# Stick-breaking attention in pairs of units: scores and scans of two units first, values one pair later, ring of four

## The chip, the cores and the metric

The kernel runs on one core of one Trainium2 chip. The metric is the device time of one execution in microseconds, as the median of several runs.

## What is computed

One layer of a streaming encoder for two requests that share the weights: a prompt of 1024 rows, and a sample of 64 new rows with 512 rows of cached keys and values. The layer is: modulation rows from a conditioning vector; a normed projection into u, q, k, v; a pooling mixer on u; stick-breaking attention with 8 heads of 64; an output projection with residual and two layer norms; a router; a mixture of 16 experts with a second residual and norm. Attention, cut to what matters:

```python
z = einsum('bqhd,bkhd->bhqk', qi, k) * scale            # scores
valid = (k_pos[None, :] < pi[:, None])[None, None]      # strictly causal
log_beta = log_sigmoid(z)
log_1m = where(valid, log_sigmoid(-z), 0.0)
suffix = cumsum(log_1m, axis=3, reverse=True) - log_1m
a = where(valid, exp(log_beta + suffix), 0.0)
attn = einsum('bhqk,bkhd->bqhd', a, v)
...
mix = concatenate([pool_out, attn], axis=-1) @ w_out
x = layer_norm(ALPHA * x + (1 + g1) * mix, ln1_g, ln1_b)
hn2 = (norm(x) * (1 + sc2) + sh2)
```

## The kernel before, in words

Three blocks follow one another: block_a (modulation, norm, projection), block_b (attention, output projection, first norm, router logits) and block_c (routing and experts). The change lies in block_b.

**How attention is computed.** The kernel doesn't form logarithms. ScalarE takes sigmoid(-z/8), which is 1 minus the stick's fraction; VectorE multiplies it up by a scan from the last key backwards (`tensor_tensor_scan`), which gives the stick that is left at each key. The weight of a key is the difference of two neighbours of that product, and the kernel moves this difference onto the values: dv holds v of a row minus v of the row before, so that left-over sticks times dv, plus the last v (vlast), is the attention.

**Units.** attention_units() lists 56 units in order: units 0 to 7 are the sample tile (per pair of heads one unit of 64 new keys and one of 512 cached ones), 8 to 23 the prompt tiles 0 to 3 with one unit for each of 4 pairs of heads (128, 256, 384, 512 keys), and 24 to 55 the tiles 4 to 7 with two units each: the upper piece (top, 128 to 512 keys, masked) and then the lower one (bottom, 512 keys), whose scan starts from what the upper left. Each unit does both heads (h = 0, 1) of its pair.

**Steps of unit u.** On TensorE (PE) scores(u) (L994) into banks 2(u%2)+h; on ScalarE (ACT) sticks(u), the sigmoid (L1135), into ring[u % RING]; on VectorE (DVE) weights(u), two scans in place (L1267 masked top, L1269 otherwise); on PE turn(u) (L1009), transposes of both heads, in blocks of 128 keys, into banks 4 and 5; on ACT copy_aT(u) (L1151), one copy a head; on PE values(u) (L1028), one matmul for each head and 128 keys, into bank 6 over the one or two units of a tile and pair of heads; on DVE, behind the last of these, copy_att(u) (L1277), with vlast added. Waits: turn(u) waits for left_ready (scan of u) and, head by head, for aT_copied of the unit before; values(u) waits for aT_copied of u and, for a top unit, for att_copied of the accumulation before; sticks(u) waits for the transposes of u - RING and for a scan.

**Order.** One loop over u on each engine, LAG = 2. PE: scores(u), turn(u-2), the other work of u, values(u-3). ACT: sticks(u), copy_aT(u-2), other work. DVE: weights(u), copy_att(u-3), other work. The other work is written out by hand in the tables PE_BESIDE, ACT_BESIDE, DVE_BESIDE, a list of steps for each u; each engine runs its own list strictly in order. The steps are: TV:n/DV (transposes of v's differences, L981, and their DVE copy L1284), PM:n (pooling map, L973, ACT copy L1140), wh:n and wl:n (high and low part of w_out, L1156 on ACT and L1289 on DVE), Ph:n and Pl:n (the same of the mixed rows, L1165, L1294), M0:n and M1:n (the halves of the output projection, 24 matmuls each, L1040), C0:n and C1:n (their DVE copies, L1305), R:n on DVE (residual, L1317), E, G, B (norm and modulation, L1325, L1341, L1358), Q1 and Q2 on ACT (squares, L1178), T0:n and T1:n (transposes of hn2, L1049, copied by H0 and H1, L1187), T2:n and R:n on PE (router, L1059 and L1068, copied by H2 on ACT and L:n on DVE, L1367), KT:n (keys transposed for output). Up to u = 57 all PE steps of the tables write bank 7 (`take` waits for the reader of the step before); in the last list (u = 58) all eight banks are used. At u = 0 and 1 PE also does turn_v(4) to (8) and DVE and ACT stage_v (v staged for output, L1237).

The lists of TensorE and the first of ScalarE (those of VectorE stand in the diff):

```python
PE_BESIDE = {
    1: "TV:0", 3: "PM:0", 4: "PM:1", 5: "TV:1", 7: "TV:2", 9: "TV:3", 10: "TV:4", 12: "TV:5", 14: "TV:6", 15: "TV:7",
    16: "TV:8", 17: "PM:2", 18: "PM:3", 19: "PM:4", 20: "PM:5", 21: "PM:6", 22: "PM:7", 23: "PM:8", 24: "PM:9",
    25: "PM:10", 26: "PM:11", 28: "M0:0", 29: "M1:0", 31: "M0:1", 33: "M1:1", 34: "T0:0", 35: "M0:2", 36: "T1:0",
    37: "M1:2", 38: "T2:0", 39: "R:0", 40: "M0:3", 41: "T0:1", 42: "M1:3", 43: "T1:1", 44: "M0:4", 45: "T2:1",
    46: "M1:4", 47: "R:1", 48: "M0:5", 49: "T0:2", 50: "T1:2", 51: "M1:5", 52: "T2:2", 53: "M0:6", 54: "R:2",
    55: "M1:6", 56: "T0:3", 57: "M0:7",
    58: "T1:3 M1:7 T2:3 T0:4 M0:8 R:3 T1:4 M1:8 T2:4 T0:5 KT:0 R:4 T1:5 KT:1 KT:2 T2:5 KT:3 KT:4 R:5 T0:6 KT:5 T1:6 KT:6 KT:7 T2:6 KT:8 R:6 T0:7 T1:7 T2:7 T0:8 T1:8 R:7 T2:8 R:8",
...
ACT_BESIDE = {
    3: "PM:0", 4: "PM:1", 12: "wh:0", 13: "wh:1", 14: "wh:2", 15: "wh:3", 16: "wh:4", 17: "PM:2 wh:5",
    18: "wh:6 PM:3", 19: "wh:7 PM:4", 20: "PM:5", 21: "PM:6", 22: "PM:7", 23: "PM:8", 24: "PM:9", 25: "PM:10",
...
```

## Time and profile before

| | us |
|---|---|
| median of 3 runs | 864.76 (864.37 to 865.07) |
| the profiled execution | 863.53 |
| span of its records | 861.8 |
| TensorE matmul busy | 792.0 (92%), 4805 matmuls |
| VectorE busy | 597.8 (69%) |
| ScalarE busy | 349.7 (41%) |
| GpSimd busy | 314.2 (36%) |
| mean granted TensorE clock | 0.968 of full speed |

The profile is one execution. Times in it are microseconds from the start of the span. Attention runs from about 243 us (first sigmoid) to 494 us (last values), the last of the output projection and the router to 533 us, then routing and experts to the end. A row of the timeline is: start, duration (several instructions merged, with their count x), engine, line, operation, tiles written and read, shapes, and in brackets how long the engine was idle before it and what ended that. The ends of matmuls are modelled, so that a group overlaps the next by some hundredths of a microsecond; the step from start to start is the surer figure.

### The profile page before, as it was taken

Reading aid. Unit: us, or ns where it says so; the run is one execution under the profiler, and the core shown is the slowest. Engines: PE = TensorE matmul, PEld = TensorE weight load, DVE = VectorE, ACT = ScalarE, POOL = GpSimd, SP = SyncE. Lnnn points to the kernel's source line nnn. Section 1 sums busy time; section 2 is a strip of 40 time slices with the busy share of each in tenths; the row PEclk is TensorE's granted clock in tenths of the full one; section 3 lists DMA queues with packets and bytes.
Section 4 is the critical chain, followed back from the end, with each engine's and each line's share of the span. In section 5 each row is a group of like instructions: output and inputs, shape, how many; then the busy total and the mean of one; then the engine's idle time right before and its main releaser. Section 6 shows DMA issues by size and latency. Waiting matters only on the chain. (4 is left out here: it accounts for less than half of the span.)

```text
span 861.8 us, 13448 instructions
## 1 busy us (share of the span) xinstructions
PE 792.0 (92%) x4805; PEld 625.4 (73%) x4806; DVE 597.8 (69%) x685; ACT 349.7 (41%) x645; POOL 314.2 (36%) x259
## 2 busy tenths in 40 slices
PE   3899999999978899999999995599999999999894
PEld 2689999999945566766767784378888888888641
DVE  6679679852079965875777566998557998563097
ACT  3811110111156763444444435544544444444144
POOL 3000799960000001000000001257665897663156
PEclk9999999999999999999999996699999999999897
DMA  8956544630073501321102037798779998889594
GB/s 322 397 175 204 163 152 132 200 98 2 1 257 144 144 17 50 100 72 38 62 26 74 25 122 265 279 327 278 272 253 334 401 384 289 278 306 345 175 355 157
DMA packets 77362, 165.32 MB, mean 192 GB/s; under 512 B 7397, under 2 KB 32517, under 8 KB 75266
## 3 DMA queue, kind: packets, MB, share of 16 engines
q1 hardware_dynamic: 68402, 132.15, 44.2%
q0 software_dynamic: 7760, 28.31, 9.3%
q10 hardware_dynamic: 1152, 4.19, 1.4%
q8 instruction: 32, 0.52, 0.3%
q14 instruction: 16, 0.13, 0.0%
HBM read 132.57 MB, written 32.08 MB: 191 GB/s over the span
## 5 line engine op out<-in xcount | busy, mean ns | idle before, releaser
L2101 PE MATMUL psum<-we_hi,x_parts 128*128 x384 | 137.5, 403 | 1.4 <-DVE we_lo L1724 1.1
L1724 DVE TENSOR_TENSOR we_lo<-we_raw,we_hi 128x2048 fp32r<-128x2048 f32 x48 | 116.1, 2422 | 1.5
L1723 DVE CAST we_hi<-we_raw 128x2048 fp32r<-128x2048 f32 x44 | 60.7, 1379 | 47.9 <-DMA we_raw<-in_w_down_dram 24.5
L449 PE MATMUL psum<-hn_hi,w_hi 128*128 128x364 f32 (+1 forms) x384 | 90.7, 331 | 1.3 <-issue 0.7
L449 PE MATMUL psum<-hn_lo,w_hi 128*128 128x364 f32 (+1 forms) x384 | 90.1, 329 | 0.0
L449 PE MATMUL psum<-hn_hi,w_lo 128*128 128x364 f32 (+1 forms) x384 | 89.9, 328 | 0.0
L2101 PEld LDWEIGHTS psum<-we_hi,x_parts 128*128 128x128 f32 x384 | 72.1, 188 | 16.5 <-issue 2.3
L1040 PE MATMUL psum<-wo_hi,mixin 128*128 128x512 f32 (+1 forms) x256 | 83.2, 396 | 0.6 <-DVE logits L1367 0.6
L2101 PE MATMUL psum<-we_lo,x_parts 128*128 x192 | 75.2, 392 | 0.0
L633 DVE SCALAR_TENSOR_TENSOR proj<-wm,cT,proj 128x2048 f32<-128x2048 f32 x28 | 72.6, 2638 | 0.1
L449 PEld LDWEIGHTS psum<-hn_hi,w_hi 128*128 128x128 f32 x384 | 67.0, 189 | 5.7 <-issue 4.8
L449 PEld LDWEIGHTS psum<-hn_hi,w_lo 128*128 128x128 f32 x384 | 67.6, 189 | 0.0
L449 PEld LDWEIGHTS psum<-hn_lo,w_hi 128*128 128x128 f32 x384 | 67.4, 189 | 0.0
L929 POOL TENSOR_TENSOR rs_x<-var_x,mhalf 128x1 f32<-128x1 f32 (+1 forms) x9 | 13.0, 1448 | 147.7 <-DVE var_x L1325 147.7
L526 ACT ACTIVATE bias<-psum 128x2 f32<-128x2 f32 x16 | 2.8, 172 | 157.1 <-PE psum L449 157.1
L1135 ACT ACTIVATE ring<-psum 128x1024 f32<-128x1024 f32 (+5 forms) x56 | 44.1, 787 | 49.2 <-PE psum L994 47.1
L1267 DVE TENSOR_TENSOR_SCAN ring<-ring,mask 128x128 f32<-128x128 f32 (+4 forms) x72 | 50.9, 747 | 9.0 <-ACT ring L1135 8.9
L1009 PEld LDWEIGHTS psum<-ident,ring 128*128 128x128 f32 (+2 forms) x328 | 34.4, 142 | 30.8 <-issue 24.0
L1821 POOL DMA_INDIRECT ff_d<-yst,idsy x24 | 50.7, 2111 | 15.6 <-ACT yst L1944 6.7
L1040 PEld LDWEIGHTS psum<-wo_hi,mixin 128*128 128x128 f32 (+1 forms) x256 | 46.3, 181 | 12.5 <-issue 1.0
L1269 DVE TENSOR_TENSOR_SCAN ring<-ring 128x512 f32<-128x512 f32 (+1 forms) x40 | 49.1, 1267 | 7.3 <-ACT ring L1135 7.3
L1040 PE MATMUL psum<-wo_lo,mixin 128*128 128x512 f32 (+1 forms) x128 | 49.9, 390 | 0.0
(334 smaller groups left out, 1587.3 us busy)
## 6 DMA issues: line engine op xcount, KB each, us to landing
we_raw<-in_w_up_dram SPq DMA_DIRECT2D x32, 1024.0 KB, 8.4
wm<-in_w_mod_dram SPq DMA_DIRECT2D x16, 1024.0 KB, 5.3
we_raw<-in_w_down_dram SPq DMA_DIRECT2D x16, 1024.0 KB, 6.6
w_raw<-in_w_in_dram SPq DMA_DIRECT2D x16, 512.0 KB, 6.2
we_raw<-ff_d SPq DMA_DIRECT2D x12, 512.0 KB, 8.3
proj<-in_x_prompt_dram SPq DMA_DIRECT2D x4, 1024.0 KB, 8.1
sc_room<-in_w_mod_dram SPq DMA_DIRECT2D x4, 1024.0 KB, 14.0
proj<-in_w_mod_dram SPq DMA_DIRECT2D x2, 2048.0 KB, 12.2
```

The costliest lines, as they stand in the source:

```text
L449: mm = pe.matmul(psum[:, 3 * slot + c, 0:n], w[:, slot, k, :], hn[:, k, t0:t0 + n], start=(k == 0 and w is w_hi and hn is hn_hi), stop=(k ...
L633: ins = dve.scalar_tensor_tensor(out=out, in0=w, scalar=c, in1=out, op0=ALU.mult, op1=ALU.add)
L929: pool.tensor_tensor(rs[of][0:r, n:n + 1], var[of][0:r, n:n + 1], mhalf[0:r, 0:1], ALU.pow).then_inc(rstd_ready[of], 1)
L1009: mm = pe.transpose(psum[0:m, 4 + h, b:b + r], ring[0:r, s, h, b:b + m], ident[0:r, 0:r])
L1040: mm = pe.matmul(out[0:r, :], mix_room(n)[:, part, k, 0:r], w[:, k, 512 * half:512 * half + 512], start=(k == 0 and part == 0 and w is wo_ ...
L1135: act.activation(ring[0:r, u % RING, :, 0:n], psum[0:r, 2 * s:2 * s + 2, 0:n], ACT.Sigmoid, scale=-0.125).then_inc(stay_ready, 1)
L1267: ins = dve.tensor_tensor_scan(w, w, mask[0:r, end - n:end][:, ::-1], first, ALU.mult, ALU.max)
L1269: ins = dve.tensor_tensor_scan(w, w, w, first, ALU.mult, ALU.bypass)
L1723: then(dve.tensor_copy(we_hi[:, a:b], raw))
L1724: dve.tensor_tensor(we_lo[:, a:b], raw, we_hi[:, a:b].bitcast(F32), ALU.subtract).then_inc(ready, 1)
L1821: pool.indirect_dma_start(ff_d, bass.IndirectOffsetOnAxis(idsy[:, s:s + 1], 0), yst[:, s, :], None).then_inc(scattered[s], 16)
L2101: mm = pe.matmul(psum[:, bank, :], x[:, s, k, :], w[:, bass.ds(at + k * 2 * DE, 2 * DE)], start=(k == 0 and x is x_hi and w is we_hi), sto ...
```

## The change

- The loops of PE and ACT go over even u and treat two units at once. PE: scores(u), scores(u+1), values(u-4), values(u-3), turn(u-2), the other work of u and of u+1, turn(u-1). ACT: sticks(u), sticks(u+1), copy_aT(u-2), other work of both, copy_aT(u-1). DVE: at even u weights(u), weights(u+1), copy_att(u-4), copy_att(u-3), then the other work of u; at odd u other work alone.
- RING goes from 3 to 4. The room comes from junk, which now shares wp's room, and zeros, which is a part of mask (one memset and one count of CONSTS less).
- The odd ones of units 8 to 23 sum their values in bank 5 (att_bank), all others in bank 6. turn(u), head 1, waits for att_copied of the odd unit before the pair where that unit used bank 5; a top unit's values wait for the last accumulation in the same bank (bank_read).
- wl:0 to wl:7 on DVE are spread over units 13 to 23; they were in 12 to 19.
- turn_v(4) to (8) follow scores(1); stage_v(8) follows stage_v(6).

```diff
@@ -143,7 +143,7 @@
         with ExitStack() as mid:
             proj = mid.enter_context(nc.sbuf_tensor("proj", [P, FC, NT], F32))
             utail = mid.enter_context(nc.sbuf_tensor("utail", [P, 4, 2, HIST], F32))
-            wp = mid.enter_context(nc.sbuf_tensor("wp", [P, 4, P], F32))
+            wp, junk = rooms(nc, mid, ("wp", [P, 4, P], F32), ("junk", [P, KC, P], BF16))
             psc = mid.enter_context(nc.sbuf_tensor("psc", [P, 4], F32))
             wgr = mid.enter_context(nc.sbuf_tensor("wgr", [P, KC, 32], F32))
             old_room = mid.enter_context(nc.sbuf_tensor("old_room", [P, 2, D], F32))
@@ -689,7 +689,7 @@
 
 UNITS = len(attention_units())
 ORDER = (PT,) + tuple(range(PT))
-RING = 3
+RING = 4
 LAG = 2
 
 
@@ -712,8 +712,8 @@
     57: "Q2:6 Ph:8 H1:3 H2:3 H0:4 Q1:7 Q2:7 H1:4 H2:4 H0:5 KT:0 H1:5 Q1:8 H2:5 KT:1 KT:2 H0:6 KT:3 H1:6 KT:4 Q2:8 H2:6 KT:5 KT:6 KT:7 H0:7 KT:8 H1:7 H2:7 H0:8 H1:8 H2:8",
 }
 DVE_BESIDE = {
-    2: "TV:0", 3: "DV:0", 5: "TV:1", 7: "TV:2", 9: "TV:3", 10: "TV:4", 12: "TV:5 wl:0", 13: "wl:1 TV:6 wl:2",
-    14: "wl:3", 15: "TV:7", 16: "TV:8 wl:4", 17: "wl:5", 18: "wl:6", 19: "wl:7", 26: "Pl:0", 28: "C0:0",
+    2: "TV:0", 3: "DV:0", 5: "TV:1", 7: "TV:2", 9: "TV:3", 10: "TV:4", 12: "TV:5", 13: "wl:0",
+    14: "TV:6", 15: "wl:1 TV:7", 16: "TV:8 wl:2", 17: "wl:3", 18: "wl:4", 19: "wl:5", 21: "wl:6", 23: "wl:7", 26: "Pl:0", 28: "C0:0",
     29: "C1:0 R:0 Pl:1", 30: "E1:0 G1:0", 31: "B1:0 C0:1 E2:0 G2:0", 32: "B2:0", 33: "C1:1 R:1 Pl:2", 34: "E1:1 G1:1",
     35: "B1:1 C0:2 E2:1", 36: "G2:1 B2:1", 37: "C1:2 R:2 Pl:3", 38: "E1:2", 39: "L:0 G1:2", 40: "B1:2 E2:2 C0:3",
     42: "C1:3 R:3 Pl:4", 43: "G2:2 E1:3 B2:2 G1:3", 44: "B1:3 C0:4", 45: "E2:3", 46: "C1:4 R:4 Pl:5 L:1", 47: "E1:4",
@@ -752,9 +752,8 @@
         k_room, mixin = one_room(nc, ctx, [P, 2, KC, P], ("k_room", F32), ("mixin", F32R))
         lT = sb("lT", [P, P])
         gather = sb("gather", [P, 32])
-        junk = sb("junk", [P, KC, P], BF16)
         mask = sb("mask", [P, 512])
-        zeros = sb("zeros", [P, P])
+        zeros = mask[:, 0:P]
         vlast = sb("vlast", [P, 4, TILES])
         edge = sb("edge", [P, 4, 2])
         sums = [sb("sums_x1", [P, TILES]), sb("sums_hn2", [P, TILES])]
@@ -813,7 +812,7 @@
         gather_made = 1
         sample_units = sum(u[0] == PT for u in units)
         EVEN = 112
-        CACHE_LOADS, EARLY_STORES, CONSTS = 16 * 4, 16 * (TILES + 2), 5
+        CACHE_LOADS, EARLY_STORES, CONSTS = 16 * 4, 16 * (TILES + 2), 4
         K_FIRST = 6
         ACT_TILES, DVE_TILES = TILES // 2, TILES - TILES // 2
 
@@ -832,6 +831,15 @@
         def v_staged(n):
 
             return (act_staged, n // 2 + 1) if n % 2 else (dve_staged, n // 2 + 1)
+
+        def att_bank(u):
+
+            return 5 if units[u][5] and units[u][6] and u % 2 else 6
+
+        def bank_read(u):
+
+            q = units[u][7]
+            return max((v[7] + 1 for w, v in enumerate(units[:u]) if v[7] < q and att_bank(w) == att_bank(u)), default=0)
 
         def mod_row(dst, b, part):
             return dst, mod_d[b, part * D:(part + 1) * D].partition_broadcast(P)
@@ -1004,6 +1011,8 @@
                 for h in range(2):
                     if u >= 1:
                         pe.wait_ge(aT_copied, 2 * u - 1 + h)
+                    if h and u >= LAG and att_bank(u - 1 - u % 2) == 5:
+                        pe.wait_ge(att_copied, units[u - 1 - u % 2][7] + 1)
                     for b in range(0, n, P):
                         m = min(P, n - b)
                         mm = pe.transpose(psum[0:m, 4 + h, b:b + r], ring[0:r, s, h, b:b + m], ident[0:r, 0:r])
@@ -1017,15 +1026,15 @@
                     pe.wait_ge(old_ready, 1)
                 else:
                     pe.wait_ge(dv_copied, ORDER.index(i) + 1)
-                if top and q:
-                    pe.wait_ge(att_copied, q)
+                if top and bank_read(u):
+                    pe.wait_ge(att_copied, bank_read(u))
                 nb = -(-n // P)
                 for b in range(nb):
                     m = min(P, n - b * P)
                     v = dv_old[0:m, b, :] if old else dv[0:m, s0 // P + b, :]
                     for h in range(2):
                         c = p * P + 64 * h
-                        mm = pe.matmul(psum[64 * h:64 * h + 64, 6, 0:r], v[:, c:c + 64], aT[0:m, s, h, b, 0:r],
+                        mm = pe.matmul(psum[64 * h:64 * h + 64, att_bank(u), 0:r], v[:, c:c + 64], aT[0:m, s, h, b, 0:r],
                                        start=(top and b == 0), stop=(bottom and b == nb - 1))
                 mm.then_inc(pv_done, 1)
 
@@ -1077,16 +1086,7 @@
 
             for n in range(4):
                 turn_v(n)
-            for u in range(nu + LAG + 1):
-                if u < nu:
-                    scores(u)
-                if 0 <= u - LAG < nu:
-                    turn(u - LAG)
-                if u >= nu:
-                    values(u - LAG - 1)
-                if u < 2:
-                    for n in ((4, 5, 6), (7, 8))[u]:
-                        turn_v(n)
+            def others(u):
                 if u == nu + LAG:
                     last_reader.update({b: [(stay_ready, nu)] for b in range(4)})
                     last_reader.update({b: [(aT_copied, 2 * nu)] for b in (4, 5)})
@@ -1106,8 +1106,28 @@
                         turn_k(n)
                     else:
                         router(n)
-                if LAG < u < nu:
-                    values(u - LAG - 1)
+
+            for u in range(0, nu + LAG, 2):
+                if u < nu:
+                    scores(u)
+                    scores(u + 1)
+                if u >= 2 * LAG:
+                    values(u - 2 * LAG)
+                    values(u - 2 * LAG + 1)
+                if u == 0:
+                    for n in range(4, TILES):
+                        turn_v(n)
+                if u >= LAG:
+                    turn(u - LAG)
+                others(u)
+                if u < nu:
+                    others(u + 1)
+                if u >= LAG:
+                    turn(u + 1 - LAG)
+            values(nu - 2)
+            values(nu - 1)
+            others(nu + 1)
+            others(nu + LAG)
 
         @block.scalar
         def _(act):
@@ -1198,13 +1218,7 @@
                 act.wait_ge(pv_done, nu)
                 act.activation(dv[0:rows(t), t, :], bank("KT", t)[0:rows(t), :], ACT.Copy).then_inc(act_staged, 1)
 
-            for u in range(nu + LAG + 1):
-                if u < nu:
-                    sticks(u)
-                if 0 <= u - LAG < nu:
-                    copy_aT(u - LAG)
-                if u < 2:
-                    stage_v(5 + 2 * u)
+            def others(u):
                 for step, n in beside(ACT_BESIDE, u):
                     if step == "PM":
                         copy_pool(n)
@@ -1221,6 +1235,23 @@
                     else:
                         copy_h(n, int(step[1]))
 
+            for u in range(0, nu + LAG, 2):
+                if u < nu:
+                    sticks(u)
+                    sticks(u + 1)
+                if u == 0:
+                    stage_v(5)
+                    stage_v(7)
+                if u >= LAG:
+                    copy_aT(u - LAG)
+                others(u)
+                if u < nu:
+                    others(u + 1)
+                if u >= LAG:
+                    copy_aT(u + 1 - LAG)
+            others(nu + 1)
+            others(nu + LAG)
+
         @block.vector
         def _(dve):
             step_ = Tally(b_dve)
@@ -1274,7 +1305,7 @@
                 i, p = units[u][0], units[u][1]
                 r = rows(i)
                 dve.wait_ge(pv_done, u + 1)
-                dve.tensor_scalar(proj[:, 4 + p, i * P:i * P + r], psum[:, 6, 0:r], vlast[:, p, i:i + 1], None,
+                dve.tensor_scalar(proj[:, 4 + p, i * P:i * P + r], psum[:, att_bank(u), 0:r], vlast[:, p, i:i + 1], None,
                                   ALU.add).then_inc(att_copied, 1)
 
             def copy_dv(n):
@@ -1367,15 +1398,18 @@
                 dve.tensor_tensor(logits[0:r, ORDER[n], :], bank("R", n)[0:r, 0:NLOG], blog[0:r, :], ALU.add).then_inc(logits_copied, 1)
 
             for u in range(nu + LAG + 1):
-                if u == 1:
-                    stage_v(8)
-                if u < nu:
-                    weights(u)
-                if u > LAG and units[u - LAG - 1][6]:
-                    copy_att(u - LAG - 1)
+                if u % 2 == 0:
+                    if u < nu:
+                        weights(u)
+                        weights(u + 1)
+                    if u >= 2 * LAG:
+                        for before in (u - 2 * LAG, u - 2 * LAG + 1):
+                            if units[before][6]:
+                                copy_att(before)
                 if u == 0:
                     stage_v(4)
                     stage_v(6)
+                    stage_v(8)
                 if u == 1:
                     dve.wait_ge(cache_loaded, CACHE_LOADS)
                     dve.tensor_tensor(dv_old[:, :, :], v_sh, dv_old[:, :, :], ALU.subtract).then_inc(old_ready, 1)
```

## Rows read from the trace of the kernel before

**Rows 1.** The page's slices: busy tenths of TensorE in 40 equal parts of the span.

```profile
PE   3899999999978899999999995599999999999894
```

**Rows 2.** Stretches of 10 us, core 0: length, PE, PEld, DVE, ACT, POOL busy, clock, DMA.

```profile
282.00:292.00 10.00, 8.93 (x70) 5.13 (x66) 10.00 (x15) 7.24 (x14) 0.00 (x0) 1.00 0.51 141
...
302.00:312.00 10.00, 10.00 (x86) 6.63 (x86) 6.86 (x11) 6.94 (x12) 0.59 (x1) 1.00 0.08 23
```

**Rows 3.** Waits of TensorE in 243 to 300 us: total, times, longest.

```profile
PE psum L1028 <- DVE proj L1277: 3.3, 4, 1.9
```

**Rows 4.** Waits of TensorE in 300 to 478 us.

```profile
PE psum L1049 <- DVE proj L1305: 3.9, 2, 2.0
PE psum L1040 <- DVE logits L1367: 0.6, 1, 0.6
PE psum L1059 <- DVE proj L1305: 0.5, 1, 0.5
```

**Rows 5.** Timeline of TensorE at several places of attention.

```profile
277.51 0.44 PE L1028 MATMUL psum<-aT_room,dv 128*64 128x128 f32 x4 [1.06 <-DVE proj L1277]
...
293.03 1.02 PE L973 MATMUL psum<-proj,wp 128*128 128x512 f32 x2
...
321.03 0.46 PE L1040 MATMUL psum<-wo_hi,mixin 128*64 128x512 f32 x1
...
397.98 0.47 PE L1040 MATMUL psum<-wo_hi,mixin 128*128 128x512 f32 x1
...
403.64 1.09 PE L1028 MATMUL psum<-aT_room,dv 128*64 128x128 f32 x16
...
404.67 1.13 PE L994 MATMUL psum<-proj 64*128 64x512 f32 x4
```

**Rows 6.** Timeline of VectorE: scans, low_wo and copy_att (272.69 is unit 12, 322.31 unit 28).

```profile
272.69 1.27 DVE L1267 TENSOR_TENSOR_SCAN ring<-ring,mask 128x256 f32<-128x256 f32 x2 [0.60 <-ACT ring L1135]
...
274.72 1.22 DVE L1289 TENSOR_TENSOR wo_lo<-wo_raw,wo_hi 128x1024 fp32r<-128x1024 f32 x1
...
277.04 0.33 DVE L1277 TENSOR_SCALAR proj<-psum,vlast 128x128 f32<-128x128 f32 x1
...
284.73 1.79 DVE L1267 TENSOR_TENSOR_SCAN ring<-ring,mask 128x384 f32<-128x384 f32 x2
...
297.69 2.33 DVE L1267 TENSOR_TENSOR_SCAN ring<-ring,mask 128x512 f32<-128x512 f32 x2
...
313.82 2.46 DVE L1269 TENSOR_TENSOR_SCAN ring<-ring 128x512 f32<-128x512 f32 x2 [1.77 <-ACT ring L1135]
...
322.31 0.71 DVE L1267 TENSOR_TENSOR_SCAN ring<-ring,mask 128x128 f32<-128x128 f32 x2
```

**Rows 7.** Timeline of ScalarE in 290 to 297 us: wo_hi, pooling copy, aT copies, sigmoid.

```profile
290.87 1.10 ACT L1156 ACTIVATE wo_hi<-wo_raw 128x1024 fp32r<-128x1024 f32 x1
291.82 0.73 ACT L1140 ACTIVATE proj<-psum,psc 128x512 f32<-128x512 f32 x1
...
293.14 0.88 ACT L1151 ACTIVATE aT_room<-psum 128x384 f32<-128x384 f32 x2
...
295.96 1.03 ACT L1135 ACTIVATE ring<-psum 128x1024 f32<-128x1024 f32 x1 [0.42 <-PE psum L994]
```

**Rows 8.** Stretches of 2 us at two gaps of TensorE, columns as in group 2.

```profile
393.00:395.00 2.00, 0.33 (x4) 0.10 (x1) 0.63 (x4) 1.81 (x3) 0.30 (x1) 1.00 0.43 130
395.00:397.00 2.00, 1.64 (x16) 1.14 (x16) 1.84 (x3) 1.80 (x4) 0.25 (x1) 1.00 0.44 133
442.00:444.00 2.00, 0.10 (x2) 0.07 (x2) 1.78 (x5) 0.69 (x1) 0.00 (x0) 1.00 0.00 0
446.00:448.00 2.00, 2.00 (x7) 0.63 (x4) 1.96 (x2) 1.43 (x3) 0.00 (x0) 0.50 0.00 0
```

**Rows 9.** Timeline of TensorE, 442 to 453 us.

```profile
443.96 0.63 PE L1049 MATMUL psum<-ident,old_room 128*128 128x128 f32 x4 [1.90 <-DVE proj L1305]
...
445.37 2.08 PE L994 MATMUL psum<-proj 64*128 64x512 f32 x4
```

More of the change, by code:

```diff
@@ L155, in build @@
             block_b(nc, ident, mhalf, psum, proj, utail, logits, fixed, mod_d, x1_d, hn2_d, x_prompt,
-                    x_sample, cache_v, old_room, wp, psc, wgr, blog, vprev, w_out, ln1_g, ln1_b,
+                    x_sample, cache_v, old_room, wp, junk, psc, wgr, blog, vprev, w_out, ln1_g, ln1_b,
                     k_prompt, v_prompt, pool_prompt, k_sample, v_sample, pool_sample)
@@ L734, in block_b @@
 def block_b(nc, ident, mhalf, psum, proj, utail, logits, fixed, mod_d, x1_d, hn2_d, x_prompt, x_sample,
-            cache_v, old_room, wp, psc, wgr, blog, vprev, w_out, ln1_g, ln1_b,
+            cache_v, old_room, wp, junk, psc, wgr, blog, vprev, w_out, ln1_g, ln1_b,
             k_prompt, v_prompt, pool_prompt, k_sample, v_sample, pool_sample):
@@ L901, in _ @@
             pool.memset(v_sh[0:1, 0, :], 0.0).then_inc(b_const, 1)
-            pool.memset(zeros[:, :], 0.0).then_inc(b_const, 1)
             pool.memset(logits[:, PT, :], 0.0).then_inc(b_const, 1)
```

## The prediction

> **What bounds the kernel now.** I read four views. First the page's 40 slices [rows 1]: TensorE is at nine tenths almost everywhere, and its one soft place before the routing is in the slices after 240 us, where attention starts. Then stretches of attention [rows 2]: from 282 to 292 us VectorE is busy 10.0 of 10 us and TensorE 8.9; from 302 us on TensorE is at 10.0 and VectorE at 6.9. So units 12 to 19 are paced by VectorE and the later ones by TensorE. The waits say the same: in 243 to 300 us TensorE waited 3.3 us for the copy of finished attention, L1277 [rows 3]; in 300 to 478 us its largest wait is 3.9 us, transposes (L1049) that found PSUM bank 7 not yet copied [rows 4]. What an exchange of order can win is thus small: 5 us of idle after 300 us, and TensorE's own cost of switching from one kind of work to the next.
>
> **Durations.** Start to start on TensorE, a unit with 512 keys takes 1.03 us for values (403.64 to 404.67) and 1.06 for scores (the transposes follow at 405.73); two pooling matmuls take 0.95, a mix half of 24 matmuls 5.66 (397.98 to 403.64) [rows 5]. VectorE, two scans: 1.19 us (256 keys), 1.71 (384), 2.25 (512, masked), 2.38 (unmasked), 0.65 (128); a step of low_wo 1.14; copy_att 0.33, start to start 0.24; copy_dv 0.66 [rows 6]. ScalarE: sigmoid 0.92 start to start (512 keys), 0.7 (384), 0.5 (256); aT copy of a head 0.28, 0.4 and 0.5; wo_hi 1.0, pooling copy 0.7 [rows 7]. A hop from VectorE to TensorE: the copy at 277.04 ends at 277.37, the values it held start at 277.51: 0.14 us [rows 5, 6]. From TensorE to another engine: about 0.28 us after the last column.
>
> **The change, part by part.**
>
> *A new wait in units 12 to 27.* The odd unit of each pair of 8 to 23 now sums its values in bank 5, the bank of head 1's transposes. So turn(u-2), head 1, waits for copy_att(u-3). TensorE comes to it right behind values(u-4) and values(u-3); but VectorE issues that copy only behind weights(u) and weights(u+1), the four scans of the pair whose scores TensorE has just made. Queued behind the waiting transpose are both units' other work, turn(u-1) and scores(u+2), for which the next scans wait. So each engine waits for the other once a pair, for u = 12, 14, ... 26. A round, from scan(u) to scan(u+2), is: four scans, two copies and the hop; then head 1's transposes, others(u), others(u+1), turn(u-1), scores(u+2), sigmoid(u+2). On ScalarE the aT copy, its own other steps and the aT copies of u-1 stand ahead of that sigmoid.
>
> Pair 20 worked out: scans 4.5, copies 0.57, hop 0.14: 5.2 us. Head 1 (three blocks of 107 ns) to 5.5; PM:5, its copy behind the aT copy, then PM:6, all in bank 7, to 7.6; turn(19) 0.84, scores(22) 1.06, 0.11 to the sigmoid, 1.05 to the scan: 10.65. Pair 12: 3.1 to head 1, aT copy to 3.65, wo_hi:0 and :1 to 5.65, two aT copies 0.35, sigmoid 0.63: 6.6. Pair 14: 3.3 after head 1, TV:6, its copy and TV:7 to 5.3, turn(13) and scores(16) to 6.85, sigmoid: 7.8. Pair 16: 4.3, then on ScalarE wo_hi, the copy of PM:2 behind TV:8, wo_hi to 7.65, aT copies and sigmoid: 9.05. Pair 18: 4.45, aT copy, wo_hi, copy of PM:3 to 6.8, PM:4 to 7.9, turn(17) 0.84, scores(20) 1.06, 1.16: 11.0. Pairs 22 and 24, with two pooling steps each: 10.1 and 10.1. Pair 26, with one and Ph:0: 7.5. Sum 72.8 us. In the kernel before, scan(12) starts at 272.69 and scan(28) at 322.31: 49.6 us for the same eight pairs [rows 6]. **+23.2.** With none of the other work in the round the rounds sum to 55, so +5 is the lower bound.
>
> *Before unit 12.* Two scans (2.8 us) now stand ahead of stage_v(4), which frees the bank for turn_v(8); low_wo's eight steps are spread over units 13 to 23 in place of 12 to 19; the large steps remain. **+0.8**, bounds -1 and +2, from no start that moves by more than a scan.
>
> *The hand-over.* Before, M0:0 starts 1.3 us ahead of scan(28), at 321.03 [rows 5, 6]. Now scores(29), values(24), values(25) and turn(26) stand between, and it starts 2.1 us behind: +3.4, less scores(29), 1.1, which is done early: **+2.3**.
>
> *Fewer switches, units 28 to 55.* Scores are 4 passes of 213 ns, 0.85 us, and take 1.06 start to start; values are 16 times 54 ns, 0.86, and take 1.03 [rows 5]. A switch to or from a kind that uses half of the array costs 0.16 to 0.21 us. A pair had six or seven of them and has three or four: I take 0.5 us a pair, 14 pairs: **-7**, bounds 0 and -9. In units 12 to 27 that gain lies in idle time. The Trainium skill (TensorE: Matmul & The Clock Gate, Step-by-step: what each phase is for) says that TensorE pulls weight loads ahead of running matmuls; if that hid every switch, this term would be 0. The rows show a cost between kinds all the same.
>
> *Other work by two, one bank.* Mix halves, transposes of hn2 and router steps all take bank 7. Between two of them stood values, scores and a turn, 3 us; now others(u) and others(u+1) are adjacent and the second waits for the reader of the first. After a mix half with a step behind it: 0.28 + 0.68 + 0.14 = 1.1, for pairs 28, 40, 42, 46, 48: 5.5. Pair 44, where VectorE reaches C0:4 late, behind B1:3: 1.5. T0:0 then M0:2 (34) waits for aT copy, square (1.25) and copy_h (0.5): 2.1; T2:0 then R:0 (38) and T2:2 then M0:6 (52) the same way, 2.1 and 1.8; T1 then M1 (36, 50) for copy_h alone, 0.9 and 1.0; R:2 then M1:6 (54) for copy_logits, now behind four scans of 4.8 us: 2.6. Sum 17.5, in place of the present 3.9 + 0.6 + 0.5 [rows 4]: **+12.5**, bounds +5 and +15.
>
> *Free edits.* zeros as a part of mask saves one memset on GpSimd, idle there. junk shares wp's room; its first write (unit 30) is behind wp's last use (unit 26). A ring of four lets sigmoid(u+1) go ahead, which the pairs need. Square's load of the next x rows, SP's loads and stores keep their order, with microseconds of slack; the tail behind M0:7 and the expert stage move as a block.
>
> *Clock.* From 442 to 444 us TensorE is busy 0.10 of 2 us, and at 446 to 448 the granted clock is 0.50 (1.2 GHz); the gap at 393 to 395, 0.33 of 2 us busy, is followed by 1.00 [rows 8]. In the first case scores at 445.37 span 2.08 us against 1.13 at full clock [rows 5, 9]. Each of the eight rounds has a gap of 2 to 3.5 us; in half of them I take a fall, 1 us each, as TensorE streams half of the round: **+4**, bounds 0 and +15. The skill's same page (Why this matters for your kernels) advises against idle gaps between bursts, which speaks against this change.
>
> **Sum.** 0.8 + 23.2 + 2.3 - 7 + 12.5 + 4 = +35.8. Against the profiled execution (span 861.8, 863.5 with what lies around it) that is 899.3, against the median 864.8 it is 900.6. I say 900.
>
> **Rivals.**
> *Light rounds* (0.22): the engines overlap more of each round than I give, the clock stays full, the bank waits are near their lower bound: 0.8 + 12 + 2.3 - 7 + 8 = +16, 881. For it: ScalarE has a third of its time free. Against: each engine's order is fixed.
> *Half clock all through* (0.13): the gaps leave TensorE at 1.2 GHz over most rounds, and bank waits bring falls of their own: +50, 915. For it: the scores at 445.37. Against: the gap at 393.
> *Switches win* (0.06, faster): if bank 5 is copied before TensorE reaches head 1's transposes, the rounds cost nothing and the gain on switches stays, with 4 us of bank waits in place of 5: 864.8 - 8 = 857. It decides where the four scans (2.4 to 4.8 us) end before scores, two values and one head (1.7 to 3.7 us); by the scan rows they don't in any of the pairs.
> *Not what it says* (0.02, within 0.2%): switches aren't saved and waits only change names: 865.
> The forecast itself has 0.57.
>
> **How the numbers follow.** The range may leave out 2 in 10: 877 to 918 holds the forecast, most of the light rounds and over half of the half-clock case. A measurement of this kernel tells about 0.2% (1.7 us) from no change. Faster 0.06, same 0.02, slower 0.92.
>
> **What would show it.** After: TensorE idle ahead of L1009 in eight places 7 to 11 us apart, ended by VectorE's copy_att; scan(12) to scan(28) near 73 us; scores of two units as one run of 8 matmuls, 1.9 us for 512 keys; waits ahead of L1040 and L1049 of about 1 us each for the readers of bank 7; tail and experts as long as before. I am wrong if those L1009 waits sum to under 10 us, or if units 28 to 55 take less time than before.

## The result: 5.9% slower

The changed kernel takes 914.8 us (median; 913.1 to 918.4), the kernel before 864.6: the ratio is 1.0589, 95% interval 1.0571 to 1.0607. The forecast was 900, range 877 to 918. The profiled execution of the changed kernel has a span of 916.6 us, 54.8 more than that of before; it is the longest one of four, so the stages below, which are cut from it, add up to 4.7 us more than the medians differ by.

In the changed kernel the lines are: scores L1001, transposes L1018, values L1037, mix L1049, hn2 transposes L1058, router L1068 and L1077, pooling map L980, sigmoid L1155, scans L1298 and L1300, copy_att L1308, copy_dv L1315, C0 and C1 L1336.

The page's slices of the changed kernel, to be laid beside [rows 1]:

```profile
PE   3899999999777768999898989469999999999894
...
DVE  6779498820375554577666637699845999664077
...
PEclk9999999999976679999999999779999999999897
```

The digits 6 to 8 of TensorE from the eleventh slice on (229 to 366 us) hold units 0 to 27 of attention; the kernel before has one 7 and two 8 there. VectorE is at 3 to 7: neither is the bound, each waits for the other. The granted clock falls to 6 and 7 tenths. Behind it TensorE is at eight and nine tenths, up to the 4 and the 6 of the routing. Two stretches of these units, up to unit 12 and units 12 to 27 (columns as in [rows 2], clock the third last):

```profile
243.00:282.00 39.00, 28.69 (x220) 18.30 (x220) 26.76 (x40) 15.35 (x39) 0.00 (x0) 0.74 0.48 182
282.00:364.00 82.00, 58.83 (x350) 35.94 (x352) 43.86 (x61) 38.80 (x68) 2.21 (x10) 0.77 0.16 42
```

The span cut at four events that both traces show (start of scan(12) and of scan(28) on VectorE, of M0:0 and M0:7 on TensorE; scan(u) is the start of unit u's scans, all in us; a negative time means that M0:0 starts first):

| stage | before | after | more | forecast |
|---|---|---|---|---|
| start to scan(12) | 272.7 | 281.9 | +9.2 | +0.8 |
| scan(12) to scan(28), eight rounds | 49.6 | 82.2 | +32.5 | +23.2, and +4 for the clock |
| scan(28) to M0:0 | -1.3 | 1.2 | +2.4 | +3.4 |
| M0:0 to M0:7 | 166.6 | 178.1 | +11.4 | +4.4 (12.5 - 7 - 1.1) |
| M0:7 to the end | 374.1 | 373.4 | -0.8 | 0 |

**The rounds.** The round of u = 20 in the changed kernel, all engines (unit 20's scans start at 321.09, unit 22's at 334.33):

```profile
321.09 4.57 DVE L1298 TENSOR_TENSOR_SCAN ring<-ring,mask 128x512 f32<-128x512 f32 x4 [6.84 <-ACT ring L1155]
...
325.58 0.58 DVE L1308 TENSOR_SCALAR proj<-psum,vlast 128x128 f32<-128x128 f32 x2
...
326.31 0.87 PE L1018 MATMUL psum<-ident,ring 128*128 128x128 f32 x3 [3.53 <-DVE proj L1308]
...
327.61 0.31 ACT L1160 ACTIVATE proj<-psum,psc 128x64 f32<-128x64 f32 x1
...
327.97 2.08 PE L980 MATMUL psum<-proj,wp 128*128 128x512 f32 x2 [0.46 <-ACT proj L1160]
...
329.84 1.49 PE L1018 MATMUL psum<-ident,ring 128*128 128x128 f32 x6
...
331.25 2.83 PE L1001 MATMUL psum<-proj 64*128 64x512 f32 x8
...
333.27 1.94 ACT L1155 ACTIVATE ring<-psum 128x1024 f32<-128x1024 f32 x2 [1.42 <-PE psum L1001]
...
334.33 2.34 DVE L1298 TENSOR_TENSOR_SCAN ring<-ring,mask 128x512 f32<-128x512 f32 x2 [7.03 <-ACT ring L1155]
```

It is the order of the forecast, step by step: four scans; copy_att twice, the last to 326.16; head 1's transposes at 326.31 after 3.53 us of idle; the copy of PM:5; PM:6; turn(19); scores(22) and (23); the sigmoid; the scan. 13.2 us, where I had worked out 10.65. What is longer are TensorE's steps alone: PM:6 1.87 from start to start in place of 0.95, turn(19) 1.41 for 0.84, scores to sigmoid 2.0 for 1.2. They run at 1.2 GHz: the granted clock of 326 to 333 us is 0.51. The waits of TensorE in 282 to 364 us:

```profile
PE psum L1018 <- DVE proj L1308: 18.7, 8, 3.5
PE psum L980 <- ACT proj L1160: 2.8, 4, 0.8
```

Eight waits for copy_att, one for each round, 1.7 to 3.5 us each and 18.7 us in all, as in the list of what would show it. They end 6.5 to 14 us apart.

**Units 28 to 55.** TensorE's waits in 365 to 543 us; [rows 4] has the same of before with 5.0 us in all:

```profile
PE psum L1058 <- DVE proj L1336: 4.0, 3, 2.3
PE psum L1049 <- ACT old_room L1207: 3.2, 3, 1.8
PE psum L1049 <- DVE logits L1398: 2.6, 1, 2.6
PE psum L1037 <- ACT aT_room L1171: 2.5, 5, 0.9
PE psum L1077 <- ACT lT L1214: 1.6, 1, 1.6
PE psum L1049 <- ACT lT L1214: 1.5, 1, 1.5
PE psum L1068 <- DVE proj L1336: 1.1, 1, 1.1
PE psum L1077 <- DVE proj L1336: 0.9, 1, 0.9
PE psum L1049 <- DVE old_room L1336: 0.9, 1, 0.9
```

Their sum is 18.3 us. Twelve of them, 15.8 us, are the twelve pairs of adjacent steps in bank 7 that the forecast lists, with 2.6 for the router's copy behind four scans (M1:6), as worked out. The other five, 2.5 us, are values (L1037) that wait for their aT copy; the forecast has no such wait. The switches are saved as well:

```profile
507.71 1.99 PE L1001 MATMUL psum<-proj 64*128 64x512 f32 x8
509.63 1.97 PE L1037 MATMUL psum<-aT_room,dv 128*64 128x128 f32 x32
511.53 0.66 PE L1018 MATMUL psum<-ident,ring 128*128 128x128 f32 x4
```

Scores of two units with 512 keys take 1.92 us from start to start, twice 1.06 before; values 1.90, twice 1.03 before [rows 5].

### The profile page after: what moved, and what is told of

It reads as the page before. It is cut to its first block and busy times, and to the rows that moved or that the text cites. A ratio compares the mean times of both kernels' runs of the same rounds, so it can differ in the third digit from the quotient of the medians.

```text
span 916.6 us, 13462 instructions
## 1 busy us (share of the span) xinstructions
PE 809.7 (88%) x4805; PEld 642.2 (70%) x4806; DVE 601.7 (66%) x685; ACT 354.8 (39%) x645; POOL 310.6 (34%) x258
## 5 line engine op out<-in xcount | busy, mean ns | idle before, releaser
L1049 PE MATMUL psum<-wo_hi,mixin 128*128 128x512 f32 (+1 forms) x256 | 84.4, 401 | 8.2 <-ACT old_room L1207 3.2
L1298 DVE TENSOR_TENSOR_SCAN ring<-ring,mask 128x128 f32<-128x128 f32 (+4 forms) x72 | 50.2, 746 | 53.6 <-ACT ring L1155 53.6
L633 DVE SCALAR_TENSOR_TENSOR proj<-wm,cT,proj 128x2048 f32<-128x2048 f32 x28 | 72.5, 2636 | 0.5 <-DMA wm<-in_w_mod_dram 0.5
L1018 PE MATMUL psum<-ident,ring 128*128 128x128 f32 (+2 forms) x328 | 52.6, 298 | 18.7 <-DVE proj L1308 18.7
L1171 ACT ACTIVATE aT_room<-psum 128x512 f32<-128x512 f32 (+4 forms) x112 | 47.3, 460 | 52.0 <-PE psum L1018 51.5
L1018 PEld LDWEIGHTS psum<-ident,ring 128*128 128x128 f32 (+2 forms) x328 | 39.7, 156 | 32.5 <-issue 29.1
L1049 PEld LDWEIGHTS psum<-wo_hi,mixin 128*128 128x128 f32 (+1 forms) x256 | 47.1, 184 | 21.2 <-issue 9.6
L1300 DVE TENSOR_TENSOR_SCAN ring<-ring 128x512 f32<-128x512 f32 (+1 forms) x40 | 49.2, 1270 | 8.1 <-ACT ring L1155 6.7
```

The lines of the kernel that those rows point to most:

```text
L633: ins = dve.scalar_tensor_tensor(out=out, in0=w, scalar=c, in1=out, op0=ALU.mult, op1=ALU.add)
L1018: mm = pe.transpose(psum[0:m, 4 + h, b:b + r], ring[0:r, s, h, b:b + m], ident[0:r, 0:r])
L1049: mm = pe.matmul(out[0:r, :], mix_room(n)[:, part, k, 0:r], w[:, k, 512 * half:512 * half + 512], start=(k == 0 and part == 0 and w is wo_ ...
L1171: act.activation(aT[0:m, s, h, 0:nb, 0:r], src, ACT.Copy).then_inc(aT_copied, 1)
L1298: ins = dve.tensor_tensor_scan(w, w, mask[0:r, end - n:end][:, ::-1], first, ALU.mult, ALU.max)
L1300: ins = dve.tensor_tensor_scan(w, w, w, first, ALU.mult, ALU.bypass)
```

## The experiments

All are edits of the changed kernel; their diffs are shortened, and ... marks what is left out. First what each came to, in us; the texts below were written before each ran. The last three columns are from one profiled execution each: the start of scan(12), the time from scan(12) to scan(28) (the eight rounds) and the time from M0:0 to M0:7.

| run | median | ratio to before (95%) | scan(12) | rounds | M0:0 to M0:7 |
|---|---|---|---|---|---|
| before | 864.6 | | 272.7 | 49.6 | 166.6 |
| the change | 914.8 | 1.059 (1.057 to 1.061) | 281.9 | 82.2 | 178.1 |
| e1_between | 887.4 | 1.027 (1.023 to 1.031) | 278.4 | 60.2 | 172.4 |
| e2_warm | 916.5 | 1.059 (1.056 to 1.062) | 282.3 | 83.3 | 176.4 |
| e3_split | 893.0 | 1.034 (1.032 to 1.035) | 277.2 | 73.9 | 164.3 |
| e4_pm | 912.5 | 1.055 (1.052 to 1.059) | 280.4 | 80.0 | 174.8 |
| e5_warm2 | 905.0 | 1.044 (1.039 to 1.048) | 279.8 | 71.3 | 174.8 |
| e6_all | 871.3 | 1.007 (1.004 to 1.009) | 276.4 | 54.4 | 163.2 |
| e7_vfirst_all | 881.9 | 1.017 (1.012 to 1.021) | 281.2 | 52.9 | 172.0 |
| e8_vfirst | 917.7 | 1.058 (1.054 to 1.063) | 281.0 | 60.8 | 197.4 |
| e9_hybrid | 861.4 | 0.996 (0.994 to 0.998) | 273.0 | 50.3 | 163.3 |
| e10_hybrid_adj | 875.0 | 1.010 (1.007 to 1.014) | 272.0 | 49.6 | 178.1 |
| e11_warm_all | 902.1 | 1.043 (1.040 to 1.047) | 275.7 | 72.5 | 176.4 |
| e12_hybrid_split | 863.3 | 0.999 (0.997 to 1.000) | 272.4 | 49.6 | 164.3 |

**Is it the copy behind four scans?** e1_between puts it between them:

```diff
                     if u < nu:
                         weights(u)
-                        weights(u + 1)
                     if u >= 2 * LAG:
...
                                 copy_att(before)
+                    if u < nu:
+                        weights(u + 1)
```

> The changed kernel with one exchange on VectorE: the two copies of finished attention stand between the scans of u and those of u+1, not behind both. Theory A (each round of units 12 to 27 is held by scans, then copy, then head 1's transposes): every round gets shorter by about one unit's scans (1.2, 1.2, 1.7, 1.7, 2.25, 2.25, 1.2, 1.2 us), 12.7 us, and by 3 to 6 more where the gap no longer halves the clock: 894 to 902 us; idle of TensorE ahead of L1018 falls from 18.7 us to under 8. Theory B (the rounds are long because TensorE runs at 1.2 GHz and ScalarE's other steps stand ahead of the sigmoid; the copy is not what is waited for): within 3 us of 914.8.

887.4: 27 us less, more than either number. The rounds are 21.9 us shorter, and their granted clock is 0.94 in place of 0.77. Theory B is out. How much of the 21.9 the copy gave and how much the clock, this run alone can't tell. With e5_warm2 (below), whose rounds take 71.3 us at 0.98 in the order of the change, it can: 11.0 us (71.3 - 60.2) for the copy's place, for 12.7 worked out, and 10.9 for the clock (with 0.98 and 0.94 neither run is quite at full clock, so both are estimates).

**What does the clock cost?** e2_warm fills TensorE's gaps with spare matmuls whose result nobody reads:

```diff
+                for _ in range(WARM.get(u, 0)):
+                    for sm, value in last_reader.get(7, ()):
+                        pe.wait_ge(sm, value)
+                    pe.matmul(psum[:, 7, :], ident[:, :], mask[:, :], start=True, stop=True)
                 if u >= LAG:
                     turn(u - LAG)
```

> The changed kernel with 41 spare matmuls of 512 columns (0.43 us each at full clock, bank 7, their result is overwritten unread) put into TensorE's gaps ahead of turn(u-2) in the rounds of u = 12 to 26, at most 3 us a round; everything else is as in the changed kernel. If the half clock in the rounds is a cost of its own beside the waits: the granted clock in 283 to 363 us rises from about 0.75 to over 0.9, and scan(12) to scan(28) falls from 82.2 us toward the 72.8 us of the forecast: 904 to 908 us. If the clock costs nothing there (the chain goes through VectorE and ScalarE): 914 to 917, or some us more where a spare matmul delays the transposes.

The clock rose to 1.00 in 283 to 363 us, and the time was 916.5. Taken by itself that would have said that the clock is free. But the trace showed each spare matmul at 0.87 us, twice what I had reckoned: those of u = 20 ended 2.0 us behind the copy that the transposes wait for, and stood in the round themselves. The next run has 18 of them in place of 41 (2 a round, 3 for u = 20 and 22):

> As the run with 41 spare matmuls, but with 18 (2 a round, 3 for u = 20 and 22), each 0.87 us by the last trace, so that they end before the copy that the transposes wait for. In the last run the spare matmuls of u = 20 ended 2.0 us behind the copy, which hid what the clock gives. If the half clock costs time of its own in the rounds (about 1 us each by the forecast, 2.4 us in the round of u = 20 by the trace): clock over 0.9 in 283 to 363 us and scan(12) to scan(28) of 70 to 76 us in place of 82.2: 902 to 909 us. If it costs nothing: 913 to 917.

905.0, and the rounds take 71.3 us, both as expected. Granted clock and busy time of 280 to 351 us, and the round of u = 20 again, now with TensorE at full clock (L1124 are the spare matmuls, copy_att is L1313, the pooling map L981, transposes L1019, scores L1002):

```profile
280.00:351.00 71.00, 60.32 (x382) 34.58 (x380) 43.79 (x61) 37.30 (x68) 2.88 (x10) 0.98 0.19 49
```

```profile
313.63 4.62 DVE L1303 TENSOR_TENSOR_SCAN ring<-ring,mask 128x512 f32<-128x512 f32 x4 [4.44 <-ACT ring L1160]
...
314.78 2.84 PE L1124 MATMUL psum<-mask,ident 128*128 128x512 f32 x6
...
318.17 0.57 DVE L1313 TENSOR_SCALAR proj<-psum,vlast 128x128 f32<-128x128 f32 x2
...
318.89 0.52 PE L1019 MATMUL psum<-ident,ring 128*128 128x128 f32 x3 [0.95 <-DVE proj L1313]
...
320.20 1.13 PE L981 MATMUL psum<-proj,wp 128*128 128x512 f32 x2 [0.61 <-ACT proj L1165]
...
321.16 0.82 PE L1019 MATMUL psum<-ident,ring 128*128 128x128 f32 x6
...
321.91 1.99 PE L1002 MATMUL psum<-proj 64*128 64x512 f32 x8
...
324.14 2.34 DVE L1303 TENSOR_TENSOR_SCAN ring<-ring,mask 128x512 f32<-128x512 f32 x2 [4.26 <-ACT ring L1160]
```

From scan to scan it is 10.51 us; the forecast's sum for it was 10.65. The eight rounds, by the starts of their scans:

| pair | 12 | 14 | 16 | 18 | 20 | 22 | 24 | 26 | sum |
|---|---|---|---|---|---|---|---|---|---|
| forecast | 6.6 | 7.8 | 9.05 | 11.0 | 10.65 | 10.1 | 10.1 | 7.5 | 72.8 |
| e5_warm2 | 6.4 | 7.6 | 9.1 | 10.7 | 10.5 | 9.8 | 9.9 | 7.2 | 71.3 |
| the change | 6.5 | 9.4 | 10.2 | 13.1 | 13.2 | 12.2 | 10.4 | 7.2 | 82.2 |

Each was sized rightly for the full clock, within 0.3 us, and the half clock adds 10.9 us (82.2 - 71.3).

**Ahead of unit 12.** The trace of the changed kernel at units 1 to 5 (L962 is turn_v(8), L1268 the copies of stage_v):

```profile
248.75 1.11 PE L962 MATMUL psum<-ident,proj 128*128 128x128 f32 x4 [3.54 <-DVE wo_raw L1268]
...
251.97 1.92 PE L1001 MATMUL psum<-k_room,proj 64*64 64x512 f32 x4
...
254.99 2.45 DVE L1300 TENSOR_TENSOR_SCAN ring<-ring 64x512 f32<-64x512 f32 x2 [1.82 <-ACT ring L1155]
257.36 0.66 DVE L1315 COPY dv<-psum 64x512 f32<-64x512 f32 x1
...
258.07 2.07 PE L980 MATMUL psum<-proj,wp 128*128 128x512 f32 x2 [3.83 <-DVE dv L1315]
...
260.08 1.11 PE L1018 MATMUL psum<-ident,ring 64*128 64x64 f32 x8
...
261.12 0.48 PE L1001 MATMUL psum<-proj 64*64 64x64 f32 x4
```

The first new wait is that of turn_v(8), 3.54 us for stage_v(4), which now stands behind the scans of units 0 and 1; in the kernel before turn_v waits 0.3. scores(2) and scores(3) stand behind it, and scores(3) starts at 251.97, in the kernel before at

```profile
248.43 1.08 PE L994 MATMUL psum<-k_room,proj 64*64 64x512 f32 x4
```

that is 3.5 us earlier. Then PM:0 (258.07) finds bank 7 only after the copy of TV:0 (257.36), which stands behind scan(3), a wait of 3.8 us for 2.4 before; turn(1) and scores(4) stand behind PM:0. e4_pm moves it, on TensorE and in the same way on ScalarE:

```diff
 PE_BESIDE = {
-    1: "TV:0", 3: "PM:0", 4: "PM:1", 5: "TV:1", 7: "TV:2", ...
+    1: "TV:0", 5: "TV:1", 6: "PM:0", 7: "TV:2", 8: "PM:1", ...
```

> The changed kernel with PM:0 and PM:1 moved from units 3 and 4 to units 6 and 8, on TensorE and ScalarE. Theory A (the 8.4 us lost before unit 12 beyond the forecast come from TensorE's queue: PM:0 waits for the copy of TV:0, which stands behind scan(3) on VectorE, and turn(1), scores(4) and scores(5) stand behind PM:0): scan(12) starts 3 to 6 us earlier than at 281.9, 909 to 912 us. Rival (the clock or VectorE's own order in 243 to 282 us): within 1.5 us of 914.8.

912.5, and scan(12) 1.5 us earlier: less than the theory had. The runs whose code is the same up to there (the change, e2_warm, e5_warm2) differ by 2.5 us among themselves. The place of PM:0 is a small part at most. e11_warm_all gives spare matmuls to that stretch too:

```diff
+                        if n == TILES - 1:
+                            pe.wait_ge(stay_ready, 1)
+                            for _ in range(3):
+                                pe.matmul(psum[:, 0, :], ident[:, :], mask[:, :], start=True, stop=True)
                         turn_v(n)
...
                     turn(u - LAG)
+                if u == 2:
+                    for _ in range(3):
+                        pe.matmul(psum[:, 6, :], ident[:, :], mask[:, :], start=True, stop=True)
```

> The run with 18 spare matmuls, with 3 more ahead of turn_v(8) (bank 0) and 3 more behind turn(0) (bank 6), where TensorE waits 3.5 and 3.8 us ahead of unit 12 in the changed kernel. If the half clock is what makes scan(12) start at 280 to 282 us (forecast 273.5): granted clock in 243 to 280 us over 0.9 in place of 0.75, scan(12) at 274 to 277 us and 899 to 902 us in all. If it is the order of the queue (PM:0 and the copies that stand behind scans): scan(12) stays at 279 to 281 and the time at 905.

scan(12) is at 275.7, within the first number, and the time 902.1. Two stretches of that run (clock third last; the changed kernel has 0.67 and 0.91 there):

```profile
253.00:263.00 10.00, 8.43 (x52) 3.84 (x50) 8.47 (x8) 4.43 (x11) 0.00 (x0) 0.96 0.78 294
263.00:273.00 10.00, 8.56 (x120) 6.72 (x122) 8.65 (x17) 4.89 (x17) 0.00 (x0) 1.00 0.33 131
```

So of the 9.2 us an estimated 4 to 6 were the clock (279.8 to 281.9 without these spare matmuls), and 3 are the order, for 0.8 forecast: with a granted clock of 0.95 from 243 us on, about the 0.94 of the kernel before, scan(12) still starts 3.0 us later than there. The other runs fit: where the granted clock from 243 us to scan(12) is 0.85 (e3_split), 0.81 (e1_between) and 0.74 (the change), scan(12) starts at 277.2, 278.4 and 281.9. No run takes away the wait of turn_v(8) alone, so its share of the 3 us isn't shown.

**Adjacent steps in one bank.** e3_split sets a turn between them, on TensorE and, in the same way, on ScalarE:

```diff
                 others(u)
+                if u >= LAG:
+                    turn(u + 1 - LAG)
                 if u < nu:
                     others(u + 1)
-                if u >= LAG:
-                    turn(u + 1 - LAG)
```

> The changed kernel with the other work of u+1 behind turn(u-1) and copy_aT(u-1), so that a turn stands between two steps that take bank 7, on TensorE and ScalarE. Theory A (adjacent steps in one bank wait for each other's reader, 17 us of waits in units 28 to 55 in place of 5, and pooling steps in the rounds): the waits fall to about 8 us and the rounds by 4 to 8 us, 895 to 903 us. Rival (these waits only take the place of others behind them, as VectorE is late in any case): 912 to 917.

893.0, 2 us under the range: 8.3 us in the rounds and 13.8 between M0:0 and M0:7, which with 164.3 us is shorter than in the kernel before. The rival is out. The clock has a part in both: it is 0.84 in the rounds for 0.77, and 1.00 behind M0:0 for 0.97, where the waits fell from 18.3 to 9.4 us.

**Without any wait for bank 5.** e8_vfirst sends the two values ahead of the scores and the copies ahead of all scans:

```diff
+                if u >= 2 * LAG:
+                    values(u - 2 * LAG)
+                    values(u - 2 * LAG + 1)
                 if u < nu:
                     scores(u)
                     scores(u + 1)
-                if u >= 2 * LAG:
-                    values(u - 2 * LAG)
-                    values(u - 2 * LAG + 1)
```

> The changed kernel with values ahead of scores on TensorE and the copies ahead of the scans on VectorE, nothing else. It takes the wait of head 1's transposes away entirely and leaves the adjacent steps in one bank. Theory A: scan(12) to scan(28) falls from 82.2 to 52 to 58 us, the 17 us of bank waits in units 28 to 55 stay: 884 to 892 us. Rival (bank waits of pooling steps and late scores hold the rounds as well): rounds over 65 us, 898 or more.

For the rounds it lies between the two numbers: 60.8 us. No wait of L1018 for copy_att is left, but 13.1 us of others are, the most for the readers of bank 7. For the whole it fails: 917.7. M0:0 to M0:7 takes 197.4 us. TensorE waits 31.7 us there for 18.3 in the change. The two largest of these waits (342 to 540 us), and one place of the timeline:

```profile
PE psum L1037 <- ACT aT_room L1171: 11.0, 11, 2.4
PE psum L1058 <- DVE proj L1336: 5.3, 3, 2.4
```

```profile
366.24 1.15 ACT L1198 ACTIVATE junk<-old_room,mean_hn 64x1024 bf16<-64x1024 f32 x1 [4.38 <-DVE mean_hn L1342]
...
367.39 1.06 ACT L1171 ACTIVATE aT_room<-psum 128x512 f32<-128x512 f32 x2
...
368.50 1.09 PE L1037 MATMUL psum<-aT_room,dv 128*64 128x128 f32 x16 [2.06 <-ACT aT_room L1171]
```

Values now come right behind turn(u-3), and their aT copy is last in ScalarE's order of the pair before, behind squares that wait for VectorE (the one at 366.24 waited 4.38 us, and the values at 368.50 waited 2.06). In the change's order the two scores stand between: its values wait 2.5 us for aT copies, here 11.0. So scores, then values, is the better order of the two between M0:0 and M0:7; what costs there is what waits for what.

**All edits together.** e6_all is between, split and the moved pooling maps; e7_vfirst_all is e8_vfirst with split and the moved maps.

> The changed kernel with all three single edits: copies between the scans of u and u+1, the other work of u+1 behind turn(u-1), PM:0 and PM:1 at units 6 and 8. If the three causes add (27 + 22 + 2 us measured singly, less 4 that the rounds share): 866 to 872 us, and what is left over the kernel before is the wait of head 1's transposes. If they overlap more (each frees the same idle time): 875 to 885.

> As the run with all three edits, but with the two values ahead of the two scores on TensorE, and both copies of finished attention ahead of all four scans on VectorE. Head 1's transposes then find bank 5 copied and the idle time ahead of L1018 is under 2 us. With the switches saved (0.5 us a pair in 14 pairs) and little else lost: 855 to 864 us, faster than the kernel before. If scores two microseconds later starve the scans instead: 866 to 875.

e6_all, 871.3: within the first number. Measured singly the three gave 27.4 + 21.8 + 2.3 = 51.5 us, together 43.5; 8 are shared. Head 1's transposes still wait 8.1 us for copy_att in its rounds. e7_vfirst_all, 881.9: neither number. Its rounds are the shorter ones, 52.9 for 54.4 us, but it starts them 4.8 us later and takes 172.0 us for 163.2 between M0:0 and M0:7. TensorE's waits there are 14.6 us for 8.5; the largest new one is of transposes (L1018) for aT copies, 4.7 us in eight places, while values wait for them 1.2 us. The rest of the 8.8 us isn't explained.

**Pairs only where TensorE is the bound.** In e6_all M0:0 to M0:7 is 3.4 us shorter than in the kernel before, and scan(28) starts 8.5 us later. e9_hybrid takes each from the better kernel:

```diff
+PAIRED = 28
...
+            for u in range(PAIRED):
+                scores(u)
+                if u >= LAG:
+                    turn(u - LAG)
...
+                others(u)
+                if u > LAG:
+                    values(u - LAG - 1)
+
+            for u in range(PAIRED, nu + LAG, 2):
                 if u < nu:
                     scores(u)
                     scores(u + 1)
...
```

> Units 0 to 27 in the order of the kernel before (one unit a step, low_wo and stage_v where they were, all values in bank 6); units 28 to 55 in pairs, with the copies between the scans of u and u+1 and the other work of u+1 behind turn(u-1). If the loss lies wholly in the rounds and in what is ahead of them, and the pairs gain by fewer switches behind unit 28 (163.3 us from M0:0 to M0:7 in the run with all three edits, 166.6 in the kernel before): scan(28) at 322 us and 860 to 863 us, 0.2 to 0.5% faster than the kernel before. If the gain of that stretch came only because other engines had got ahead in a slower start: 864 to 867.

861.4, ratio 0.9961 (0.9944 to 0.9977): 0.4% faster than the kernel before, with an interval that stays under 1. The three largest of its waits in 320 to 485 us (L1059 hn2 transposes, L1069 router, L1050 mix):

```profile
PE psum L1059 <- DVE proj L1350: 2.2, 2, 1.5
PE psum L1069 <- DVE proj L1350: 1.7, 1, 1.7
PE psum L1050 <- DVE logits L1412: 1.1, 1, 1.1
```

e10_hybrid_adj pairs the same units in the order of the change itself, and e12_hybrid_split differs from e9_hybrid only in that the copies stand behind all four scans:

> As the hybrid, but behind unit 28 in the order of the change itself: other work of u and u+1 adjacent, copies behind all four scans. It prices the pairs of units 28 to 55 alone. Expected by the forecast's steps 12.5 - 7, and by the trace of the changed kernel 178.1 us for 166.6: M0:0 to M0:7 in 174 to 179 us, 873 to 878 us. If the adjacent steps cost only because the clock fell or VectorE came late out of the rounds: under 868.

> The hybrid (pairs from unit 28 on, other work of u+1 behind turn(u-1)) with the copies of finished attention behind all four scans, as the change has them. If the place of the copies matters only where bank 5 or a top unit waits for them: M0:0 to M0:7 as in the hybrid, 163 us, and 860 to 863 us. If late copies hold values or the mix there: 864 to 867.

e10_hybrid_adj, 875.0 and 178.1 us from M0:0 to M0:7, to the tenth what the changed kernel has: its loss there is its own and doesn't come from the slow start. e12_hybrid_split, 863.3, between its two numbers: as fast as the kernel before, and 1.9 us behind e9_hybrid, with ratios whose intervals just overlap, and 164.3 us for 163.3 between M0:0 and M0:7. Where the copies stand matters little once nothing waits for bank 5.

## Why the forecast was right, and where it wasn't

The range held the time and the mechanism was the one forecast. It isn't luck of terms that cancel: nearly all misses go one way, and the time lies near the upper end of the range, which had been drawn to hold part of the half-clock rival. By its steps:

- *The new wait.* Right in kind, place and size: eight waits of L1018 for copy_att, 18.7 us; each round at full clock within 0.3 us of what was worked out, 71.3 for 72.8 in all. Taking only the copy out of the way (e1_between) gave 22 us in the rounds, 11 of them without the clock's part.
- *Clock.* The term that was mis-sized. I took +4, half of the rounds with 1 us each. It is 10.9 in the rounds (82.2 against 71.3), and by the estimates here 4 to 6 ahead of unit 12 and 3.4 between M0:0 and M0:7, for which the sum had no term: 18 to 20 us in all. In the rounds the granted clock is 0.77 of full speed on average, so nearly half of that time ran at 1.2 GHz. I had judged by two single gaps [rows 8], where TensorE was busy before and after. Here a gap of 1.7 to 3.5 us comes every 6.5 to 14 us, and the steps between two gaps are slower, which makes the round longer. The rival with the half clock all through, at 915, had the time almost to the point, though only part of its way: the bank waits of units 28 to 55 brought just three falls.
- *Before unit 12.* Forecast +0.8, bounds -1 to +2; 3 at full clock and 9.2 as it ran, outside the bounds. The step that failed: I saw that two scans now stand ahead of stage_v(4) and so of turn_v(8), but not that scores(2) and scores(3) stand behind turn_v(8) on TensorE. scores(3) came 3.5 us later, and VectorE waited for its sigmoid (1.82 us at 254.99), then at all but one of the pairs up to unit 12.
- *Hand-over.* +2.4 for +3.4; the 1.1 of scores(29) shows in the next stage.
- *Switches.* A run of scores or of values saves what was worked out (1.92 and 1.90 us). For the stretch as a whole, an estimate: 178.1 less 18.3 of waits, less 5.1 for the clock (TensorE stood at 1.2 GHz for 10.2 us in the three falls, and half of that is lost), is 154.7; before it was 166.6 - 5.0 - 1.7 = 159.9. That is 5.2 less, 1.1 of it scores(29): -4.1 for -7. e9_hybrid, at full clock with 8.6 us of waits between M0:0 and M0:7, gives the same (163.3 - 8.6 = 154.7). So the term was some 3 us too large; which of the switches with hn2 transposes and router steps between the turns cost again wasn't tried. A run of eight score matmuls saves 0.20 us against two runs of four. That weight loads are pulled ahead of running matmuls, as the Trainium skill has it (TensorE: Matmul & The Clock Gate, Step-by-step: what each phase is for), doesn't hide the switch here.
- *One bank.* Twelve waits, 15.8 us for 17.5, in place of 5.0: +10.8 for +12.5. The values' five waits for aT copies, 2.5 us, had no term. e3_split took 13.8 us off the stage, some 9 of them waits and the rest the clock, which is at 1.00 there.
- *Free edits, tail, experts.* -0.8 us, as said.

The profiled executions differ by 54.8 us for 35.8 forecast. The misses: 8.4 ahead of unit 12; in the rounds 6.9 for the clock, less 1.5 for the rounds themselves; 7.0 between M0:0 and M0:7 (by the estimates above, with rounding: waits 0.8, switches 2.9, falls of the clock 3.4); -1.0 at the hand-over and -0.8 at the end. That is 19.0.

## What to carry over

When two units are taken together, every wait between them has to be read again with both units' work in front of it: a bank or a buffer that one engine frees behind its whole double step is a rendezvous once a pair, and steps that were spaced by other work and share one bank become a chain. Pair only where the engine that is to gain is the bound; here units 28 to 55 were paired (e9_hybrid), and it gave 0.4%. Judge what a wait costs TensorE with the clock in it: size the round at full clock, then ask how often the gap comes back.

## Not expected of the hardware

Gaps of 1.7 to 3.5 us that return every 6.5 to 14 us, with shorter ones between them, held TensorE near half of its time at 1.2 GHz (0.77 granted in 282 to 364 us), and 18 spare matmuls, 15.7 us of work that nobody reads, made the kernel 9.8 us faster. The price of the half clock was 10.9 us on eight rounds of 71.3. The Trainium skill advises against idle gaps between bursts of matmuls (TensorE: Matmul & The Clock Gate, Why this matters for your kernels); the trace agrees.
